# Sample attention of a hybrid decoder step: ten key tiles per sequence in place of twelve, and cached keys that come from the host already turned

## The reference, cut to what matters

```python
DILATED = ((128, 1), (512, 4), (2048, 16))
def dilated_attention_sample(q, kc, vc):        # q (8, 8, 8, 64), kc and vc (8, 2048 + 8, 8, 64)
    ...
    for window, dil in DILATED:
        j = jnp.arange(window // dil + 1)
        idx = W + ti[:, None] - dil * j[None, :]
        valid = idx >= 0
        ...
        s = jnp.einsum('bthd,btjhd->bthj', q, kg, preferred_element_type=jnp.float32)
        s = jnp.where(valid[None, :, None, :], s, -jnp.inf)
        mx = jnp.max(s, axis=-1, keepdims=True)
        p = jnp.exp(s - mx)
        ...
    return combine_by_denominator(outs, lses)
```

## Time and profile before

| | |
|---|---|
| time, median of 3 runs | 2793.16 us (2788.93, 2793.16, 2793.8) |
| span of the profiled execution | 2790.8 us |
| busy: PE, DVE, ACT, POOL | 96%, 65%, 39%, 25% of the span |
| `mix_sample` on PE | from 1076.8 us to 1246.5 us of the span |

### The profile page before, as it was taken

How to read it: one execution, slowest core, us unless ns; L and a number is a source line. 1 busy time by engine, 2 the same in 40 slices (tenths; PEclk the granted TensorE clock), 3 DMA queues, 4 the chain that set the end, 5 groups by cost and what they waited for, 6 DMA issues and landing times. The chain is left out here.

```text
span 2790.8 us, 45736 instructions
## 1 busy us (share of the span) xinstructions
PE 2667.3 (96%) x17331; PEld 2256.3 (81%) x17331; DVE 1806.6 (65%) x3848; ACT 1075.5 (39%) x1975; POOL 692.4 (25%) x585
## 2 busy tenths in 40 slices
PE   7999999999899998989989999899999999999997
PEld 6888888878777776768877888799998888778886
DVE  6722566333688885567667676755655766887778
ACT  4312332010566774333346555555553211221113
POOL 1167212120245453112210000100002434333332
PEclk9999999999999999989999999999999999999999
DMA  5367543254454547967846777778869777786672
GB/s 184 140 214 265 198 145 143 107 178 139 138 174 155 172 142 290 399 263 261 303 164 209 269 270 269 263 269 298 278 234 335 271 243 255 265 310 225 220 266 87
DMA packets 342705, 628.68 MB, mean 225 GB/s; under 512 B 38431, under 2 KB 241315, under 8 KB 326742
## 3 DMA queue, kind: packets, MB, share of 16 engines
q1 hardware_dynamic: 273132, 530.24, 54.8%
q10 hardware_dynamic: 68218, 91.51, 9.1%
q0 software_dynamic: 1152, 4.19, 0.4%
HBM read 455.36 MB, written 237.61 MB: 248 GB/s over the span
## 5 line engine op out<-in xcount | busy, mean ns | idle before, releaser
L3573 DVE TENSOR_TENSOR mlp_acc<-mlp_acc,bank 128x512 f32<-128x512 f32 x440 | 299.6, 685 | 143.4 <-PE bank L2861 137.1
L2859 PE MATMUL bank<-mlp_wd,mlp_u_hi 128*128 128x512 f32 x896 | 350.5, 391 | 8.9 <-DVE mlp_acc L3573 5.1
L2861 PE MATMUL bank<-mlp_wd,mlp_u_lo 128*128 128x512 f32 x896 | 349.2, 390 | 0.0
L2860 PE MATMUL bank<-mlp_wd,mlp_u_hi 128*128 128x512 f32 x896 | 349.1, 390 | 0.0
L3342 ACT ACTIVATE mlp_u_hi<-mlp_u_raw 128x768 fp32r<-128x768 f32 x126 | 113.1, 945 | 445.4 <-POOL mlp_u_raw L3210 445.0
L2859 PE MATMUL bank<-mlp_h_hi,mlp_wu_hi 128*128 128x272 f32 x896 | 259.3, 289 | 9.3 <-DVE mlp_h_lo L3431 4.8
L2860 PE MATMUL bank<-mlp_h_lo,mlp_wu_hi 128*128 128x272 f32 x896 | 258.8, 289 | 0.0
L2861 PE MATMUL bank<-mlp_h_hi,mlp_wu_lo 128*128 128x272 f32 x896 | 257.9, 288 | 0.0
L292 PE MATMUL p_bank<-p_w_hi,p_hT_hi 128*128 128x512 f32 x640 | 250.4, 391 | 5.2 <-DVE p_stage L836 5.1
L294 PE MATMUL p_bank<-p_w_hi,p_hT_lo 128*128 128x512 f32 x640 | 249.1, 389 | 0.0
L293 PE MATMUL p_bank<-p_w_lo,p_hT_hi 128*128 128x512 f32 x640 | 249.1, 389 | 0.0
(11 more groups left out here) (448 smaller groups left out, 6104.4 us busy)
## 6 DMA issues: line engine op xcount, KB each, us to landing
mlp_wd<-wd SPq DMA_DIRECT2D x31, 2048.0 KB, 8.1
mlp_wd<-wd SPq DMA_DIRECT2D x32, 1536.0 KB, 7.3
mlp_u_raw<-u SPq DMA_DIRECT2D x256, 128.0 KB, 2.4
out_win_k_sample<-in_cache_k SPq DMA_DIRECT2D x48, 680.0 KB, 8.9
out_win_v_sample<-in_cache_v SPq DMA_DIRECT2D x48, 680.0 KB, 9.6
mlp_wu_raw<-in_w_up SPq DMA_DIRECT2D x31, 1024.0 KB, 6.0
p_w_raw<-in_w_tok SPq DMA_DIRECT2D x10, 2048.0 KB
wd<-mlp_un_hi SPq DMA_DIRECT2D x21, 896.0 KB, 4.5
```

What stands on the lines that cost most here:

```text
L2859: nc.tensor.matmul(out, ah, bh, start=fresh and k == 0, stop=False, skip_group_check=not fresh)
L2860: nc.tensor.matmul(out, ah, bl, start=False, stop=False, skip_group_check=not fresh)
L2861: ins = nc.tensor.matmul(out, al, bh, start=False, stop=k == n - 1, skip_group_check=not fresh)
L3573: v.tensor_tensor(a, a, b[:], ALU.add).then_inc(summed, 1)
```

## The change

The rows are chosen anew, so that none is loaded twice. Ten tiles per sequence stay: the 8 tiles with the first 8 of every 16 rows as before, and 2 tiles with the other 8 of every 16 rows of the last 512. The table is made to match, over 1280 cached positions instead of 1536. The host also lays out the chosen keys turned (`cache_kt`: sequence, 128 head columns of a pair, 4 pairs, 1280 positions). One DMA per sequence brings them, with 20 KB on each partition, and `scores` reads them from where they land. The transposes of the keys, the two PSUM copies per pair of tiles and `sm_kT` go (its space is kept). Values are still loaded by rows, in two DMAs: 16 KB on a partition as before, and 4 KB in place of 8 KB. Waits on "keys of b turned" become waits on the third chunk of scores of b. The third chunk is 256 wide.

```diff
-KT = 13
-OLD = 12 * P
+WT = 10
+KT = WT + 1
+OLD = WT * P
...
+def sample_key_columns(cache):
+
+    p = np.arange(P)
+    late = WB - 512 + 16 * (p % 32) + 8 + 2 * (p // 32)
+    pos = np.concatenate([16 * p + r for r in range(8)] + [late + y for y in range(2)])
+    return cache[:, pos, :].reshape(DEC_B, OLD, H // 2, P).transpose(0, 3, 2, 1)
+
+def load_keys(sp, dst, turned, b, landed):
+    sp.dma_start(dst[:], turned[b]).then_inc(landed, 16)
+
 def load_window(sp, dst, cache, b, landed):
     sp.dma_start(dst[:, 0:8], cache[b].rearrange("(i r) c -> i r c", r=16)[:, 0:8]).then_inc(landed, 16)
-    sp.dma_start(dst[:, 8:12], cache[b, WB - 512:WB, :].rearrange("(i r) c -> i r c", r=4)).then_inc(landed, 16)
+    sp.dma_start(dst[:, 8:WT], cache[b, WB - 512:WB, :].rearrange("(i z a y) c -> z a i y c", z=2, a=4, y=2)[1]).then_inc(landed, 16)
...
             def load_k(b):
-                load_window(sp, kin[b % 2], K.ins["cache_k"], b, k_in[b % 2])
+                load_keys(sp, kin[b % 2], K.ins["cache_kt"], b, k_in[b % 2])
...
                 if b + 2 < DEC_B:
-                    sp.wait_ge(s["turned"], T.turned("k", b, 11))
+                    sp.wait_ge(s["scores"], 4 * b + 3)
                     load_k(b + 2)
...
-            pool.wait_ge(s["turned"], T.turned("k", 0, 11))
+            pool.wait_ge(s["scores"], 3)
             for h in range(MH):
                 pool.dma_start(by_head[:, :, h, 0:MD], K.ins["state_C"][:, h].rearrange("b d e -> d b e")).then_inc(s["C_in"], 16)
...
-            pool.wait_ge(s["turned"], T.turned("k", 6, 11))
+            pool.wait_ge(s["scores"], 4 * 6 + 3)
...
             def scores(b, ci):
                 n = 4 * b + ci
-                w = 512 if ci < 3 else NS
-                if ci < 3:
-                    after(pe, T.out("k", b, 4 * ci + 2))
-                    after(pe, T.out("k", b, 4 * ci + 3))
+                w = min(512, OLD - 512 * ci) if ci < 3 else NS
                 if n >= 2:
                     pe.wait_ge(s["masked"], n - 1)
                 for c in range(PAIRS):
-                    src = kT[:, (3 * b + ci) % 2, c, :] if ci < 3 else knT[:, c, :]
+                    src = kin[b % 2][:, c, 512 * ci:512 * ci + w] if ci < 3 else knT[:, c, :]
                     ins = mm(bank[SC[n % 2]][QW * c:QW * (c + 1), 0:w], qz[:, b, c, :], src, start=True, stop=True)
...
             def first_half(b, groups=None):
                 if b:
-                    pe.wait_ge(k_in[b % 2], 32 * ((b + 1) // 2))
+                    pe.wait_ge(k_in[b % 2], 16 * ((b + 1) // 2))
                 for ci in range(3):
-                    keys(b, ci)
                     if ci:
                         scores(b, ci - 1)
```

More of the change, by code:

```diff
@@ L1411, in _ @@
                     sp.wait_ge(s["staged_turned"], 2 * NCH)
-                    load_window(sp, K.k_first, K.ins["cache_k"], 0, s["next_in"])
+                    load_keys(sp, K.k_first, K.ins["cache_kt"], 0, s["next_in"])
                     load_sample_rows(K, sp, s["next_in"])
@@ L1954, in sample_tables @@
     p = np.arange(P)
-    pos = np.concatenate([16 * p + r for r in range(8)] + [WB - 512 + 4 * p + c for c in range(4)]
-                         + [WB + np.arange(DEC_T)])[None, :]
+    late = WB - 512 + 16 * (p % 32) + 8 + 2 * (p // 32)
+    pos = np.concatenate([16 * p + r for r in range(8)] + [late + y for y in range(2)] + [WB + np.arange(DEC_T)])[None, :]
+    assert len(set(pos[0].tolist())) == pos.size
     back = WB + t - pos
     n = OLD + DEC_T
[L1959 to L1965, removed]
+    assert pos.shape[1] == n
+    d16 = (back >= 0) & (back % 16 == 0) & (back <= 2048)
+    d4 = (back >= 0) & (back % 4 == 0) & (back <= 512)
+    d1 = (back >= 0) & (back <= 128)
     count = d16.astype(np.float32) + d4 + d1
@@ L1993, in __init__ @@
         for b in range(DEC_B + 1):
-            if b < DEC_B:
-                order += [("k", b, x) for x in range(12)]
             if b:
@@ L2087, in mix_sample @@
         assert -(-nc.sbuf_base // 32) * 32 == K.front_at + 4 * TOP
-        sb("kin_home", [P, 12, AW])
-        later = [12 * AW]
+        sb("kin_home", [P, HOME, AW])
+        later = [HOME * AW]
         def front(name, *shape):
@@ L2249, in _ @@
                 act.wait_ge(K.hb_out[p], 16 * (NCH // 2))
[L2251 to L2258, removed]
             def exps(b):
@@ L2318, in bc @@
                 return ap.rearrange("p (h a) -> p h a", a=1).broadcast_to([NS, MH, w])
-            def keys(b, ci):
-                for x in (4 * ci + 1, 4 * ci + 3):
-                    n = 3 * b + ci
-                    dve.wait_ge(s["turned"], T.turned("k", b, x))
-                    if x % 4 == 1 and n >= 2:
-                        dve.wait_ge(s["scores"], 4 * ((n - 2) // 3) + (n - 2) % 3 + 1)
-                    v.tensor_copy(kT[:, n % 2, :, P * (x % 4):P * (x % 4 + 1)],
-                                  bank[T.bank("k", b, x)][:].rearrange("p (h c) -> p h c", h=PAIRS)).then_inc(s["copied_d"], 1)
             def masked(b, c):
                 p, n = b % 2, 4 * b + c
-                w = 512 if c < 3 else NS
+                w = min(512, OLD - 512 * c) if c < 3 else NS
                 dve.wait_ge(s["scores"], n + 1)
@@ L2462, in open_group @@
                 return bank[T.bank(kind, b, i)]
-            def keys(b, ci):
-                p = b % 2
-                for x in range(4 * ci, 4 * ci + 4):
-                    dst = open_group("k", b, x)
-                    for c in range(PAIRS):
-                        ins = tp(dst[:, P * c:P * (c + 1)], kin[p][:, x, P * c:P * (c + 1)], ident[:])
-                    ins.then_inc(s["turned"], 1)
             def scores(b, ci):
                 n = 4 * b + ci
-                w = 512 if ci < 3 else NS
-                if ci < 3:
-                    after(pe, T.out("k", b, 4 * ci + 2))
-                    after(pe, T.out("k", b, 4 * ci + 3))
+                w = min(512, OLD - 512 * ci) if ci < 3 else NS
                 if n >= 2:
@@ L2503, in second_half @@
                     if i < 3:
-                        for k in range(4):
+                        for k in range(min(4, WT - 4 * i)):
                             x = 4 * i + k
@@ L3760, in sb @@
             return ctx.enter_context(K.nc.sbuf_tensor("shared_" + name, shape, F32))
-        K.k_first, K.k_second = K.place("k_first", 0, [P, 12, AW]), K.place("k_second", TOP, [P, 12, AW])
+        K.k_first, K.k_second = K.place("k_first", 0, [P, H // 2, OLD]), K.place("k_second", TOP, [P, H // 2, OLD])
         K.C = sb("C", [P, MH, MD + 1])
```

39 lines of the change are left out of this document (20 added, 19 removed).

## The result

The changed kernel takes 2800.61 us (median of 5 runs, 2797.52 to 2803.06), the kernel before 2789.08 (5 runs on the same chip, 2786.76 to 2793.8). The ratio is 1.0047, with a 95% interval of 1.003 to 1.0064: it is slower, by 8 to 18 us. (Ratios stand here as they were recorded; the quotient of two medians can differ from them by 0.001.) I had predicted 2765, a range of 2753 to 2778, and given "slower" 3%. Both the range and the sign are wrong.

The account below looks back on a forecast made before the run. PE was taken to set the pace at 14.3 us a sequence, the fetch just behind. Fetch-limited gain 27 us plus 1.4 behind it, 28.4 us: from 2793.2 to 2764.8, say 2765 us, range 2753 to 2778.

Parts of the forecast that it names:

- The 4 KB pieces are one fifth of the values: Late value load: its small pieces noted only as a fifth of the values, with 399 GB/s taken for loads.
- Unknown costs: Loads with 20 KB on a partition, unmeasured: bounds 364 and 424 GB/s, 399 taken; products from landed buffers priced as from sm_kT.
- What would show it: Signs: right, DMA share 1.00 to about 1190 us; wrong, late key landings or SP waiting for stores behind values of 5.
- What goes from PE: PE's work per sequence: 7.3 us against 14.30, 7.0 us less for each of 8 sequences, 56 us in all.
- the pace passes from PE to the fetch: Each sequence: fetch at 13.1 us is above PE's 7.3, so only part of the 56 us can come.
- What goes from the DMAs: Keys and values of a sequence: 2.62 MB each instead of 3.15, so 5.24 MB, 13.1 us at 399 GB/s.
- How far the fetch has to run: Loads up to the values of 6: 41.9 MB plus dry spells; second_half(6) ends at 1192.5, 27 us earlier than 1219.6.
- Behind it: Next stage's first tile, after second_half(6): DVE's weights and blend done early while PE waits, giving 1.4 us.
- Slower: Rival: the keys' 20 KB runs come at half rate, 200 GB/s, 39 us more less 28.4: 2804 us; 3%.
- Nothing gained, as when a piece costs by its count: Rival: the fetch keeps 15.8 us a sequence, pieces costing by count and not bytes: 2793 us; 3%.
- The clock: PE slows after waits: 1.5 us each taken on the path; rival with 2.4 us for six sequences, 2777 us, 14%.
- The rule that the prediction quoted: Skill page on HAM oscillation: a loop with compute per slice shorter than its load wait starts every slice at half clock.

Follow-up runs that it names:

- e2: Changed kernel with late value rows dealt to other partitions, so one load has 32 outermost, not 4; key columns and tables follow: 2767.91 us, ratio 0.9935.
- e1: Changed kernel with the late value load split into four loads of 32 partitions, same bytes and places: 2771.65 us, ratio 0.9949 to the kernel before.
- e6: e2 with twelve tiles and the row grouping of before: keys turned by the host, no byte saved: 2786.97 us, ratio 1.0003.
- e5: Kernel before with ten tiles, late rows of keys and values dealt out as in e2, keys still turned on chip: 2774.02 us, ratio 0.9958.
- e8: e2 with state products and numerators moved behind second_half(1), and GpSimd's second weight quarter held until DVE blended the first tile: 2762.2 us, ratio 0.9917.
- e3: Changed kernel with each sequence's keys loaded in two DMAs, 16 KB and 4 KB on a partition, instead of one of 20 KB: 2800.81 us, ratio 1.0058.
- e12: e8 with the carried state's four loads on SP's queue ahead of the keys of sequence 2, not on GpSimd's queue: 2761.02 us, ratio 0.9902.
- e4: Kernel before with the last 512 rows of keys and values dealt out with 4 outermost, same bytes: 2962.81 us, ratio 1.0628.
- e10: e2 with the values too laid out by the host, one 20 KB run on each partition: 2778.78 us, ratio 0.9955.

## Why the prediction was wrong

**The step that failed** is "The 4 KB pieces are one fifth of the values", in "Unknown costs". Piece size was all I asked about this load. The load itself stood in the order of instructions with its source's outermost dimension of 4, and I priced it as if its bytes were spread as those of any other. So the term of the sum that failed is the rate of 399 GB/s, 13.1 us a sequence: from 1080 to 1220 us the changed kernel moved 299 GB/s at a share of 0.87. The page "DMA: Bandwidth & Descriptors" of the Trainium skill states the rule, in the section "Why a DMA increments its semaphore by 16 and not by 1": the number of engines is the largest, up to 16, that divides the outermost dimension (other than 1) of both sides; I overlooked it. The trace agrees (a share of 0.28 and 114 GB/s).

With the engines counted one by one, the prediction's own sum comes near the result. Four engines carry (5.24 - 0.52) / 16 + 0.52 / 4 = 0.426 MB of a sequence, not 0.328: 17.1 us at 25 GB/s, not 13.1. Over the seven sequences ahead of second_half(6) that is 28 us, all that I had found to gain. 2765 + 28 = 2793; measured 2800.6. Beside it the trace shows two things that this sum leaves out. Pieces are longer: 20 KB took 913 ns on average (807 in e2), the late 4 KB pieces 227 (164). And SP stood for stores queued behind the values of 5, the gap that "What would show it" named. On SP's queue `k_second` (keys 7) is issued, and the next row is 20.8 us later:

```profile
1175.81 0.48 SPq L2029 DMA_DIRECT2D k_second<-in_cache_kt  x1
1196.58 0.39 SPq L1806 DMA_DIRECT2D out_pt<-parts  x1
...
1198.02 0.43 SPq L2033 DMA_DIRECT2D sm_vin<-in_cache_v  x1
```

In e2 this gap is 11.4 us, in the kernel before 6.3.

That the sum comes so near is in part luck. Here is an estimate from the packets of three traces, from 5 us behind the start of the stage to the last row of second_half(6). "Idle" is the engines' idle time as a share of all 16. "Longer" is what pieces of 4, 8, 16 and 20 KB took above 0.162, 0.308, 0.612 and 0.764 us, in total, divided by 16.

| kernel | length | idle | longer | MB moved |
|---|---|---|---|---|
| as changed | 150.5 us | 19.0 us | 22.4 us | 46.0 |
| e1 | 121.9 us | 1.9 us | 16.8 us | 43.8 |
| e2 | 113.5 us | 5.7 us | 5.0 us | 43.7 |

Against e1, 17 us of the 29 are engines that stood idle, as the count of engines has it. Against e2 these are 13 us, and 17 more are longer pieces, for which the sum has no term. They are longer in e1 too, where the load is even, so four engines are not their only cause. In the times e1 and e2 are only 4 us apart, since e2 lost 6 of its 8 us behind second_half(6).

**What goes from PE** held. Its busy time fell as computed, and e6 shows that by itself it is worth nothing, as "the pace passes from PE to the fetch" had it. **What goes from the DMAs** holds when the load is even: e5, with the bytes alone, gains 11.7 us.

**How far the fetch has to run**, for an even kernel: e2 moved 405 to 418 GB/s from 1140 to 1200 us, where I took 399, and its stage up to second_half(6) shrank by 24 us, not 27. The difference lies at the carried state, where its products took 9.32 us and not 7.2 plus 1.5, and the engines nearly empty for some 5 us from 1118, where I had 3.

**Behind it** was wrong in sign, even for an even kernel. I had taken DVE's work on the first tile as done early, -1.4 us; GpSimd's work came to lie on top of it, and PE waited 3.1 us longer than before. In e8, without the second collision, PE waits 1.7 us less than before, near the 1.4 of that term.

**The rivals.** "Slower" had the right place to look, a load at less than its full rate, but named the keys' 20 KB runs, which e3 clears; that its 2804 us is close to the measured 2800.6 is luck. "Nothing gained, as when a piece costs by its count" is cleared by e2, with the same pieces. **The clock** is paid in both: after the waits, the value products take 4.49 or 4.50 us for 2.39 in the changed kernel and in e2 (at 1183.03), and e2 is still 18 us faster than before. The mean granted clock up to the end of second_half(6) is 0.76 in the changed kernel and 0.83 in e2: PE waits more, and so runs more at 1.2 GHz. What part of the 33 us between them that is, no run separates. The rule that the prediction quoted speaks of a loop with less work than wait; it did not fit the prediction's own numbers, 7.3 us of work to 5.8 of waiting.

## To carry to other kernels

Before pricing a load by bytes, look at the outermost dimension of both its patterns: a slice written with 4 outermost ran on four engines here, and held up all that was queued behind it. In a profile this is a DMA share that rests at 0.2 to 0.3 while work is queued. When a change makes one engine's wait disappear, look at which other work now falls together, here GpSimd and DVE on the next stage's first tile. Small packets that a whole stage waits for are worth trying ahead of the large ones in the same queue, not beside them in another: in e12 the wait for them went, though the gain in time is within the noise.

## What was not expected of the hardware

- While a four-engine load runs, pieces of other loads take longer too: 16 KB pieces 723 ns on average in the changed kernel and 622 in e8 (913 against 641 in e4 and before). In e1, where the load is spread evenly but neighbouring pieces still lie 32 KB apart in memory, the 4 KB pieces took 260 ns, and 164 in e2, where they lie side by side in fours. In e1 pieces of 20 KB were longer too, 857 ns against 807 in e2 and 913 in the changed kernel. So an uneven load is not needed for it. e1 differs from e2 in the distance, in the number of loads and in the partitions that each writes; no run separates these.
- Larger pieces are not always better: 20 KB in place of 16 and 4 KB pushed the landing of the state back (e10), and the median is 11 us above that of e2.
- On SP's queue the state went in pieces of 512 bytes (4132 of that size in e12), on GpSimd's in pieces of 4 KB (1024), and still each of its loads landed 6.7 to 8.4 us after its issue, where they took 14 to 29 us in e8.
- An operation of DVE on 24 elements took 4.39 us beside one of GpSimd (e2), for 0.20 alone.
